# A hybrid of state-space, attention and delta-rule layers: the gated linear units of both state-space layers as seven half-size products, and three smaller changes

## The chip, the core and the metric

The kernel runs on one core of one Trainium2 chip. The metric is the device time of one execution in microseconds (us); lower is better. The kernel before takes 4232.0 us, the median of three runs (4231.37 to 4232.86). All numbers are 32-bit floats. TensorE (PE) multiplies, VectorE (DVE), ScalarE (ACT) and GpSimd (POOL) do the rest, SyncE (SP) starts most weight loads.

## The reference

512 tokens of width 2048 pass through two layers of a first block and one layer of a second block.

```python
for l in range(2):                                  # the first block
    mod = silu(c) @ w_ada[l] + b_ada[l]             # shift, scale, gate: 6144 columns
    h = rms_norm(x, norm_g[l]) * (1 + scale) + shift
    u, z_s, q, k, v, z_a = split(h @ w_in[l])       # each 1024 wide
    y = gelu(state_space(u))                        # 512 x 1024
    ab = y @ w_glu[l] + b_glu[l]                    # 1024 x 2048: the gated linear unit
    y_s = ab[:, :1024] * sigmoid(ab[:, 1024:]) * silu(z_s)
    y_a = diff_attention(rope(q), rope(k), v) * silu(z_a)
    x = x + gate * (concat(y_s, y_a) @ w_out[l])
...
# the second block: one layer, its own modulation
q_a, k_a, v_a, z_a, b_a, a_a, q_b, k_b, v_b, z_b, gl_a, gl_b = split(h @ w_in_2)
beta = sigmoid(b_a)                                 # 8 heads: 8 columns
g = -exp(a_log) * softplus(a_a + dt_bias)           # 8 columns
...                                                 # gated delta rule, in chunks
bias = rel_bias[t5_bucket(dist)]                    # 16 heads, a band of 128 distances
logits = where(valid, q_b @ k_b.T * scale + bias, -inf)   # sliding window
```

## The kernel before

The program is planned first: generators append steps to one list, and every engine then walks this list and issues its own part of each step in the list's order. So the order is written out by hand, through generators that are interleaved at fixed rates, and each engine's queue is in order: an instruction that waits holds up all that stand behind it on its engine.

Activations lie transposed in two regions (features on partitions, 512 tokens along). A weight block of 1 MB goes into one of four slots (`wring`). A matrix product is a job for 256 output columns. `dense` (L539) computes it as two tiles of 128 columns by 512 tokens, each a chain of matmuls over the 128-row pieces of the inner dimension. `fast` (L491) computes the same job from seven products of half size (128 columns by 256 tokens over half of the inner dimension) instead of eight; PE takes them in the order 1, 2, 4, 6, 5, 7, 3 (`seventh`, L1478). DVE makes for it four sums of weight halves (`w_sum`, L1957), which product 7, products 5 and 6, and product 3 need, per operand once the sums of its quarters (`quarter_sums`, L2006), and puts the products together (`fold`, L1980) in six operations; product 7 also waits for the first fold. ACT copies one product out between (`set_by`). In the kernel before, `fast` is used for the output projection of layer 1 and for most of the second block; the gated linear unit uses `dense`.

A 32-bit matmul is two instructions in the profile, so that 256 instructions of 128x512 are the 128 matmuls of one layer's unit.

The unit (`glu`, L1003) has eight jobs per layer, in pairs: one for 256 gate columns (ACT takes the Sigmoid of each tile, DVE multiplies with z) and one for the matching output columns (DVE multiplies them by the gate). They stand at the end of `beside_attention` (L931), the filler that is interleaved with `attention` (L949) at 1.6 filler steps per attention step for the first 32 steps and then 45/37. A filler step is what a job issues between two `yield`s: for `dense` four matmuls of 128x512, for `fast` one half-size product. The attention handles 8 heads with four query blocks each ("units"); one unit has two steps: PE makes the scores (`k,q`), DVE masks and takes the maximum (`soften`), ACT the exponential, DVE weighs the two maps (`weigh`), PE transposes the weights (`const,tring`).

At each filler step `carry` (L464) also moves the modulation of later layers (`modulation`, L600) on by 1.7 of its steps: POOL fetches a piece of `w_ada` into `side`, DVE adds it times c into a sum (`ada_sum`, a SCALAR_TENSOR_TENSOR `tring<-side,cact,tring`), and when a sum over 16 pieces is complete PE adds it over the partitions: four matmuls with a single column of ones (`ada_turn`, L1532) into a bank that the modulation holds until its end.

The second block begins with two groups of conv products. Then come 16 columns for b_a and a_a as a job of their own (`ba`): ACT copies the result, PE turns it, ACT takes the Sigmoid, DVE computes the decay (`gates`, L2451). After it come the window's values (`vb`, 64 matmuls of 128x256 with the tokens on the output's partitions), and then products for the delta rule, with one step of `make_band` (L1102) per product: for each of 16 heads PE spreads a column of `rel_bias` over 128 partitions and 384 distances, DVE adds the mask and POOL stores it.

## Time and profile before

| | |
|---|---|
| median of three runs | 4232.0 us |
| the profiled execution | 4236.4 us |
| its span | 4234.6 us |
| PE busy | 4106.9 us, 97% of the span |
| DVE busy | 2264.3 us, 53% |
| ACT, POOL busy | 811.7 us, 498.3 us |

The profile is of one execution. Busy time is the time in which an engine executes; PE's matmuls are pipelined, so the mean duration of one is longer than the distance between two. The chain that ended last is 87% PE and 8% DVE.

### The profile page before, as it was taken

The numbers are of one execution on the slowest core, as the hardware profiler recorded it, in microseconds if no ns is written. First come the engines' busy times: TensorE is split into PE (matmuls) and PEld (weight loads), VectorE is DVE, ScalarE is ACT, GpSimd is POOL, SyncE is SP. The second block draws the span as 40 slices with busy tenths as digits, with TensorE's granted clock in tenths as the row PEclk, the third lists the DMA queues.
The fourth block names the chain that finished last, engine by engine and source line by source line (L and its number), as shares of the span: only waits on it lengthen the run. The fifth ranks groups of instructions, "written<-read, shape, count | busy, mean of one in ns | idle before, by whom it ended". The sixth has DMA issues, their size and how long they took to land.

```text
span 4234.6 us, 41304 instructions
## 1 busy us (share of the span) xinstructions
PE 4106.9 (97%) x16042; PEld 2753.4 (65%) x16042; DVE 2264.3 (53%) x4157; ACT 811.7 (19%) x1481; POOL 498.3 (12%) x816
## 2 busy tenths in 40 slices
PE   6999999999999999999999999999999999999999
PEld 3665544444446555444458757888888888888888
DVE  5666536664523664355656535555555347665643
ACT  2222201132011222011221222222221123320000
POOL 0243111111111332111111000000000011100000
PEclk8999999999999999999999999999999999999999
DMA  9533332434552333324345232121212243424423
GB/s 327 197 120 105 109 127 94 130 110 152 149 168 86 114 105 112 127 92 129 109 144 167 92 123 82 60 75 60 75 60 75 75 131 125 140 87 150 133 95 105
DMA packets 370193, 499.29 MB, mean 118 GB/s; under 512 B 44380, under 2 KB 279119, under 8 KB 369487
## 3 DMA queue, kind: packets, MB, share of 16 engines
q1 hardware_dynamic: 289984, 340.16, 24.8%
q0 software_dynamic: 38608, 125.86, 9.4%
q10 hardware_dynamic: 41406, 30.63, 2.3%
q8 instruction: 127, 2.08, 0.2%
q14 instruction: 68, 0.55, 0.0%
HBM read 462.51 MB, written 34.08 MB: 117 GB/s over the span
## 4 chain that ended last, share of the span: by engine, by line
PE 87%; DVE 8%; ACT 2%; DMA 2%; issue 1%; ACTq 0%; POOL 0%; DVEq 0%; SPq 0%; POOLq 0%
PE bank L108 84%; PE bank L111 2%; DVE tring L123 2%; DVE tring L129 2%; ACT tring L116 1%; DMA side<-in_w_ada 1%; DVE wring L123 1%; DVE bank L123 0%; DVE dring L123 0%; DVE tring L126 0%; ACT L116 0%; DVE dring L126 0%; DVE s_delta L123 0%; DMA yaT<-in_w_ada 0%; ACT L120 0%
## 5 line engine op out<-in xcount | busy, mean ns | idle before, releaser
L108 PE MATMUL bank<-region_b,wring 128*128 128x256 f32 (+2 forms) x4448 | 1322.6, 451 | 5.0 <-ACT region_b L116 3.9
L108 PEld LDWEIGHTS bank<-region_b,wring 128*128 128x128 f32 (+1 forms) x4448 | 829.5, 190 | 409.4 <-issue 330.1
L108 PE MATMUL bank<-region_a,wring 128*128 128x256 f32 (+1 forms) x3232 | 1070.9, 484 | 1.6 <-DVE wring L123 1.6
L108 PEld LDWEIGHTS bank<-region_a,wring 128*128 128x128 f32 x3232 | 604.7, 191 | 384.3 <-issue 338.7
L153 POOL DMA_DIRECT2D side<-in_w_ada x384 | 209.0, 545 | 1306.1 <-DVE tring L129 937.0
L129 DVE SCALAR_TENSOR_TENSOR tring<-side,cact,tring 128x512 f32<-128x512 f32 x360 | 302.9, 841 | 78.2 <-DMA side<-in_w_ada 41.3
L123 DVE TENSOR_TENSOR tring<-bank,tring 128x256 f32<-128x256 f32 (+1 forms) x229 | 101.0, 441 | 317.9 <-PE bank L108 314.8
L108 PE MATMUL bank<-wring,region_b 128*128 128x512 f32 (+1 forms) x640 | 263.5, 568 | 7.2 <-ACT region_b L116 7.2
L123 DVE TENSOR_TENSOR wring<-wring 128x1024 f32<-128x1024 f32 (+1 forms) x213 | 234.8, 1102 | 19.8 <-PE bank L108 10.9
L108 PE MATMUL bank<-wring,region_a 128*128 128x512 f32 x512 | 227.9, 603 | 4.4 <-ACT region_a L116 4.4
L116 ACT ACTIVATE tring<-bank 128x512 f32<-128x512 f32 (+1 forms) x166 | 81.3, 492 | 777.9 <-PE bank L108 470.3
L108 PEld LDWEIGHTS bank<-wring,region_b 128*128 128x128 f32 x640 | 150.3, 238 | 113.8 <-issue 84.8
L123 DVE TENSOR_TENSOR tring<-bank,side 32x512 f32<-32x512 f32 (+1 forms) x160 | 110.1, 688 | 175.2 <-PE bank L108 171.2
L116 ACT ACT_TABLE_LOAD x111 | 142.4, 1283 | 308.4 <-DVE sring L126 252.4
L108 PEld LDWEIGHTS bank<-wring,region_a 128*128 128x128 f32 x512 | 126.6, 250 | 97.5 <-issue 67.9
L108 PE MATMUL bank<-yaT,wring 128*128 128x512 f32 (+1 forms) x512 | 170.6, 486 | 0.0
L123 DVE TENSOR_TENSOR bank<-bank,tring 128x256 f32<-128x256 f32 (+1 forms) x213 | 110.2, 517 | 84.2 <-PE bank L108 81.7
L123 DVE TENSOR_TENSOR tring<-tring 128x512 f32<-128x512 f32 (+2 forms) x142 | 98.7, 695 | 88.8 <-ACT tring L116 83.2
L116 ACT ACTIVATE tring<-bank,sring 128x128 f32<-128x128 f32 (+3 forms) x128 | 67.3, 526 | 410.9 <-DVE sring L126 410.8
L108 PEld LDWEIGHTS bank<-yaT,wring 128*128 128x128 f32 x512 | 97.1, 190 | 66.9 <-issue 60.3
L116 ACT ACTIVATE tring<-tring 128x512 f32<-128x512 f32 x145 | 88.0, 626 | 254.7 <-DVE tring L126 189.6
L111 PEld LDWEIGHTS bank<-const,tring 128*128 128x128 f32 (+1 forms) x474 | 55.8, 142 | 77.0 <-issue 45.5
(285 smaller groups left out, 4312.0 us busy)
## 6 DMA issues: line engine op xcount, KB each, us to landing
wring<-in_w_in SPq DMA_DIRECT2D x180, 1024.0 KB, 5.3
side<-in_w_ada POOLq DMA_DIRECT2D x384, 256.0 KB, 3.2
wring<-in_w_out SPq DMA_DIRECT2D x48, 1024.0 KB, 8.5
yaT<-in_w_ada SPq DMA_DIRECT2D x16, 1024.0 KB, 9.3
wring<-in_w_glu SPq DMA_DIRECT2D x16, 1024.0 KB, 8.1
tring<-x_saved SPq DMA_DIRECT2D x48, 256.0 KB, 2.9
gring<-in_w_ada POOLq DMA_DIRECT2D x43, 256.0 KB, 3.0
SS<-in_w_ada SPq DMA_DIRECT2D x8, 1024.0 KB, 9.5
```

The lines of the kernel that those rows point to most:

```text
L108: return self.e.matmul(*a, **k) if self.e else self
L111: return self.e.transpose(*a) if self.e else self
L116: return self.e.activation(o, x, f, **k) if self.e else self
L123: return self.e.tensor_tensor(*a) if self.e else self
L129: return self.e.scalar_tensor_tensor(out=o, in0=a, scalar=s, in1=b, op0=op0, op1=op1) if self.e else self
L153: return self.e.dma_start(dst, src, allow_slow_non_contiguous=True) if self.e else self
```

## The change

1. The gated linear units of both layers use `fast`. The operand's quarters are summed into the region of h, which is free once the layer's last projection is done (`lambda: [full(last, 1)]`). The rates of `interleave` and `carry` are as before, while a job now has seven filler steps where it had four.
2. `ada_turn` transposes the sum (four transposes) into a bank of its own, and DVE adds along the free axis (`ada_total`).
3. The 16 columns for b_a and a_a are fetched beside the 256 of the values, whose matmuls become 272 wide; `gates` moves behind them.
4. The band of all 16 heads is made by a single matmul (a partition for each of 16 heads, eight times over), one addition and eight stores.

```diff
-        return 4 if self.n > 256 else 8
+        return 4 if self.width > 256 else 8
+
+    @property
+    def width(self):
+        return self.n + (self.more[1] if self.more else 0)
...
             def turn(n0):
+                aux.take("ada_turn", m, n0)
                 do("ada_turn", m, n0)
                 temps.give("acc", m, n0)
+
+            def total(n0):
+                do("ada_total", m, n0)
+                aux.give("ada_turn", m, n0)
...
         def glu(l):
             wg = d["w_glu"][l]
 
+            last = len(jobs) - 1
+            parts = Split(f"glu{l}", HT, lambda r, k, n: xTs[l][:, HT + HT // 2 * r + k:HT + HT // 2 * r + k + n, :], lambda k: [ssm_d.of("yT", l, k)],
+                          [pairs_of(hTs[l][:, 2 * i:2 * i + 2, :]) for i in range(4)], lambda: [full(last, 1)], {})
+            quarter(parts, 0, 4)
+            do("quarter_rest", parts, 0, 4)
+
             def y_dense(n0, use):
-                return Dense(wg, HT, n0, 256, False, lambda k: xTs[l][:, HT + k, :], lambda k: [ssm_d.of("yT", l, k)], use, (l, n0 % HALF // P))
+                return Dense(wg, HT, n0, 256, False, None, parts.ready, use, (l, n0 % HALF // P), parts, lay[l]["s3_glu"])
...
-                yield from dense(y_dense(HALF + n0, "glu_gate"))
-                yield from dense(y_dense(n0, "glu_out"))
+                yield from fast(y_dense(HALF + n0, "glu_gate"))
+                yield from fast(y_dense(n0, "glu_out"))
...
-        run_all(dense(layer_dense(2, w_two, OFF["ba"], "keep_ba", n=2 * GH)))
...
-        do("gates")
...
+        vb_job = layer_dense(2, w_two, OFF["vb"], "keep_v2", tokens="blocks")
+        vb_job.more = (OFF["ba"], 2 * GH)
+        run_all(dense(vb_job))
+        do("gates")
...
-        interleave(gdn_products(0, 2), make_band(), 1)
+        aux.take("band")
+        temps.take("band")
+        do("band")
+        aux.give("band")
+        temps.give("band")
+        run_all(gdn_products(0, 2))
...
             def ada_turn(m, n0):
...
-                    i = pe.matmul(bank[:, c:c + 1], acc[:, j * P:(j + 1) * P], ones[:, 0:1], start=True, stop=True)
+                    i = pe.transpose(bank[:, j * P:(j + 1) * P], acc[:, j * P:(j + 1) * P], ident)
...
+            def band_():
+                place = temps.at("band")
+                room(aux.clear("band"))
+                pe.wait_ge(*att_d.of("rel_bias"))
+                pe.matmul(aux.at("band")[:, 0:SW_W], place[0:32, SW_W:SW_W + P], K("hot")[0:32, :], start=True, stop=True).then_inc(
+                    *scored.up("band"))
...
+            def ada_total(m, n0):
+                bank, l, c = aux.at("ada_turn", m, n0), mods[m][0], n0 // P
+                dve.wait_ge(*ada_turned.of(m, n0))
+                dve.reduce_sum(mod[:, l, c:c + 4], bank[:, :].rearrange("p (j k) -> p j k", j=4), AX).then_inc(*ada_ready.up("total", m, n0))
...
             def gates_():
+                dve.wait_ge(*taken_a.of("beta", TT - 1))
...
             def keep_v2(jid, j, l):
                 dve.wait_ge(*full(jid, j))
...
+                dve.tensor_tensor(gates[:, 7, j, :], bank[:, 256 + GH:256 + 2 * GH], hp[:, 1, :], AD).then_inc(*taken_d.up("decay_in", j))
+                dve.tensor_copy(temps.at("vb", j)[:, 0:256], bank[:, 0:256]).then_inc(*taken_d.up("vb", j))
...
+            def keep_v2(jid, j, l):
+                room(passed("h2"))
+                act.wait_ge(*taken_d.of("vb", j))
+                act.activation(gates[:, 1, j, :], banks.at(jid, j)[:, 256:256 + GH], ACT.Sigmoid).then_inc(*taken_a.up("beta", j))
...
+                for r in range(8):
+                    pool.dma_start(band_dram[:, 16 * r:16 * r + 16, :], temps.at("band")[16 * r:16 * r + 16, 0:SW_W].unsqueeze(1).broadcast_to(
+                        [16, 16, SW_W])).then_inc(*band_out.landing())
```

How the change moves instructions is seen in the order in which they stand on an engine. A row is the operation, output<-inputs, the shape and how many of the same follow each other; here a matmul counts once.

PE at the start of layer 0's gated linear unit, before (`region_a` holds its operand, `const,tring` are the transposes of attention weights, `k,q` its scores):

```order
L108 MATMUL bank<-region_a,wring 128x512 x4
L111 MATMUL bank<-const,tring 128x128 x2
L108 MATMUL bank<-region_a,wring 128x512 x8
L108 MATMUL bank<-k,q 128x512 x2
L108 MATMUL bank<-region_a,wring 128x512 x4
L111 MATMUL bank<-const,tring 128x128 x3
```

The same place after (`region_b` holds the sums of quarters, `s_glu` the weights of product 7):

```order
L108 MATMUL bank<-region_a,wring 128x256 x4
L111 MATMUL bank<-const,tring 128x128 x2
L108 MATMUL bank<-region_a,wring 128x256 x4
L108 MATMUL bank<-region_b,wring 128x256 x4
L108 MATMUL bank<-k,q 128x512 x2
L108 MATMUL bank<-region_b,wring 128x256 x4
L111 MATMUL bank<-const,tring 128x128 x3
```

Between two attention instructions about as many filler steps stand as before, each with half the columns.

DVE at that place before, from the end of the last finished head (`yaT`) to the next unit's mask (`const_one`):

```order
L129 SCALAR_TENSOR_TENSOR yaT<-tring,vec,yaT 128x512
L129 SCALAR_TENSOR_TENSOR tring<-side,cact,tring 128x512
L123 TENSOR_TENSOR tring<-tring 128x512
L129 SCALAR_TENSOR_TENSOR tring<-side,cact,tring 128x512 x2
L138 RECIPROCAL sring<-sring 128x1 x2
L126 TENSOR_SCALAR tring<-tring,sring,small 128x384
L129 SCALAR_TENSOR_TENSOR tring<-tring,sring 128x384
L123 TENSOR_TENSOR bank<-bank,const_one 128x128
```

And after:

```order
L129 SCALAR_TENSOR_TENSOR yaT<-tring,vec,yaT 128x512
L123 TENSOR_TENSOR region_b<-region_a 128x1024
L123 TENSOR_TENSOR region_b<-region_a,region_b 128x1024 x2
L123 TENSOR_TENSOR region_b<-region_a 128x1024
L123 TENSOR_TENSOR s_glu<-wring 128x512
L123 TENSOR_TENSOR wring<-wring 128x4x128
L129 SCALAR_TENSOR_TENSOR tring<-side,cact,tring 128x512
L123 TENSOR_TENSOR wring<-wring 128x4x128
L129 SCALAR_TENSOR_TENSOR tring<-side,cact,tring 128x512
L123 TENSOR_TENSOR wring<-wring 128x4x128
L129 SCALAR_TENSOR_TENSOR tring<-side,cact,tring 128x512
L138 RECIPROCAL sring<-sring 128x1 x2
```

Four sums of quarters and four sums of weights stand between the head's end and the weighing of the next unit (RECIPROCAL and what follows it).

PE between the conv products and the first delta-rule products of the second block, before (`tring,ones` are sums of squares for a norm):

```order
L108 MATMUL bank<-tring,ones 128x512
L108 MATMUL bank<-region_b,wring 16x512 x4
L111 MATMUL bank<-const,tring 128x16 x4
L108 MATMUL bank<-wring,region_b 128x256 x64
L108 MATMUL bank<-region_b,wring 128x256 x8
L108 MATMUL bank<-const_two,relb 128x384
L108 MATMUL bank<-region_b,wring 128x256 x8
L108 MATMUL bank<-const_two,relb 128x384
```

After:

```order
L108 MATMUL bank<-tring,ones 128x512
L108 MATMUL bank<-wring,region_b 128x272 x4
L108 MATMUL bank<-tring,ones 128x512
L108 MATMUL bank<-wring,region_b 128x272 x52
L108 MATMUL bank<-const_two,tring 128x384
L108 MATMUL bank<-region_b,wring 128x256 x16
L108 MATMUL bank<-region_a,wring 128x256 x16
```

The job of 16 columns and 15 of 16 band matmuls are gone; the one that is left stands ahead of the products, behind the gates.

## Rows read from the trace of the kernel before

**Rows 1.** The page's busy times: busy us, share of the span, instructions.

```profile
PE 4106.9 (97%) x16042; PEld 2753.4 (65%) x16042; DVE 2264.3 (53%) x4157; ACT 811.7 (19%) x1481; POOL 498.3 (12%) x816
```

**Rows 2.** Stretches: from:to length, busy us (instructions) of each engine, PE clock, DMA.

```profile
895.80:1038.20 142.40, 140.00 (x385) 63.26 (x384) 75.70 (x165) 46.79 (x83) 17.39 (x31) 1.00 0.46 148
2066.20:2204.90 138.70, 136.65 (x385) 63.33 (x384) 75.95 (x165) 47.23 (x83) 16.82 (x30) 1.00 0.48 152
905.35:1002.00 96.65, 96.51 (x270) 42.93 (x269) 55.34 (x132) 39.47 (x71) 10.74 (x20) 1.00 0.44 144
```

**Rows 3.** PE's timeline, layer 0's unit: start, us, operation, instructions [idle before].

```profile
901.78 0.41 PE L111 MATMUL bank<-const,tring 128*128 128x128 f32 x2 [2.27 <-DVE tring L129]
1006.41 0.60 PE L111 MATMUL bank<-const,tring 128*128 128x128 f32 x4
...
1016.73 17.33 PE L108 MATMUL bank<-region_a,wring 128*128 128x512 f32 x40
1033.90 0.95 PE L108 MATMUL bank<-ones,tring 128*128 128x1 f32 x8
```

**Rows 4.** PE's timeline in the last projection, which is made of half-size products.

```profile
4099.15 10.52 PE L108 MATMUL bank<-mixed,wring 128*128 128x256 f32 x48
4109.51 3.62 PE L108 MATMUL bank<-mixedT,wring 128*128 128x256 f32 x16
```

**Rows 5.** Groups of DVE instructions by form, 3500 to 4000 us: busy, mean ns, idle before.

```profile
L123 DVE TENSOR_TENSOR tring<-bank,tring 128x256 f32<-128x256 f32 x73 | 30.9, 423 | 65.0 <-PE bank L108 64.2
L123 DVE TENSOR_TENSOR wring<-wring 128x512 f32<-128x512 f32 x42 | 29.1, 692 | 3.4
L123 DVE TENSOR_TENSOR bank<-bank,tring 128x256 f32<-128x256 f32 x49 | 20.8, 425 | 21.4 <-PE bank L108 21.4
L123 DVE TENSOR_TENSOR bank<-bank,tring 128x512 f32<-128x512 f32 x24 | 16.8, 699 | 0.8
L123 DVE TENSOR_TENSOR region_b<-region_a,region_b 128x1024 f32<-128x1024 f32 x2 | 2.5, 1226 | 0.1
```

**Rows 6.** DVE's timeline in both units.

```profile
905.42 0.75 DVE L129 SCALAR_TENSOR_TENSOR tring<-side,cact,tring 128x512 f32<-128x512 f32 x1
...
911.88 0.69 DVE L144 TENSOR_REDUCE sring<-bank 128x1 f32<-128x512 f32 x1
...
999.74 0.75 DVE L129 SCALAR_TENSOR_TENSOR region_a<-bank,vec,tring 128x512 f32<-128x512 f32 x1 [2.45 <-PE bank L108]
...
1001.25 0.75 DVE L129 SCALAR_TENSOR_TENSOR tring<-tring,sring 128x512 f32<-128x512 f32 x1
...
2073.96 0.75 DVE L129 SCALAR_TENSOR_TENSOR yaT<-tring,vec,yaT 128x512 f32<-128x512 f32 x1
```

**Rows 7.** ACT's timeline in layer 0's unit.

```profile
904.73 1.28 ACT L116 ACT_TABLE_LOAD   x1
906.03 0.69 ACT L116 ACTIVATE tring<-bank,vec 128x512 f32<-128x512 f32 x1
```

**Rows 8.** PE's timeline at the head of the second block.

```profile
2469.99 1.02 PE L108 MATMUL bank<-tring,ones 128*128 128x512 f32 x2
...
2485.55 1.10 PE L108 MATMUL bank<-tring,ones 128*128 128x512 f32 x2 [0.49 <-ACT tring L116]
...
2491.28 27.89 PE L108 MATMUL bank<-wring,region_b 128*128 128x256 f32 x128
2519.01 3.62 PE L108 MATMUL bank<-region_b,wring 128*128 128x256 f32 x16
...
2583.02 1.06 PE L108 MATMUL bank<-gates,const_two 128*128 128x8 f32 x8
```

**Rows 9.** DVE's timeline at the gates and behind them.

```profile
2492.42 0.19 DVE L123 TENSOR_TENSOR gates<-bank,headp 128x32 f32<-128x32 f32 x1 [3.66 <-ACT gates L116]
...
2498.80 0.19 DVE L129 SCALAR_TENSOR_TENSOR gates<-gates,headp 128x32 f32<-128x32 f32 x1
...
2519.67 2.36 DVE L123 TENSOR_TENSOR region_b<-region_b 128x1024 f32<-128x1024 f32 x2
```

More of the change, by code:

```diff
@@ L626, in modulation @@
                         turn(n0 - 512)
+                    if k == 8 and n0 > blocks[0]:
+                        total(n0 - 512)
             for _ in range(10):
@@ L1100, in build @@
         w_two = d["w_in_2"][0]
-        def make_band():
-            for h in range(16):
-                aux.take("band", h)
-                temps.take("band", h)
-                do("band", h)
-                aux.give("band", h)
-                temps.give("band", h)
-                yield
         def conv_job(h0, which):
@@ L1465, in mm @@
                     if job.tokens:
-                        i = pe.matmul(bank[:, 0:job.n], job.rhs(k, j), blk[:, k - k0, 0:job.n], start=k == 0, stop=k == job.kt - 1)
+                        i = pe.matmul(bank[:, 0:job.width], job.rhs(k, j), blk[:, k - k0, 0:job.width], start=k == 0, stop=k == job.kt - 1)
                     else:
@@ L1706, in values @@
                 t.then_inc(*valued.up(l, h))
-            def band_(h):
-                room(aux.clear("band", h))
-                pe.wait_ge(*two_in.all())
-                pe.wait_ge(*const_two_in.all())
-                pe.matmul(aux.at("band", h)[:, 0:SW_W], relb[0:32, h:h + 1].broadcast_to([32, P]), K("hot")[0:32, :], start=True,
-                          stop=True).then_inc(*scored.up("band", h))
-            def ba_turn():
-                bank, ba = aux.at("ba_turn"), temps.at("ba")
-                room(aux.clear("ba_turn"))
-                pe.wait_ge(*taken_a.of("ba_tile"))
-                for j in range(TT):
-                    i = pe.transpose(bank[:, 2 * GH * j:2 * GH * (j + 1)], ba[0:2 * GH, J[j]], ident[0:2 * GH, 0:2 * GH])
-                i.then_inc(*turned.up("ba"))
-                temps.leave(("ba",), pe.mine())
+            def band_():
[4 more added lines that the diff above has]
+                    *scored.up("band"))
             def gate_sums():
@@ L3058, in two_constants @@
                 act.dma_start(const_two[:, :], d["const"][:, split:]).then_inc(*const_two_in.landing())
-            def keep_ba(jid, j, l):
-                room(passed("h2"))
-                room(temps.clear("ba"))
-                act.wait_ge(*full(jid, j))
-                act.activation(temps.at("ba")[0:2 * GH, :], banks.at(jid, j)[0:2 * GH, :], ACT.Copy).then_inc(*taken_a.up("ba_tile"))
-                banks.leave((jid, j), act.mine())
-            def ba_turn():
-                bank = aux.at("ba_turn")[:, 0:2 * GH * TT].rearrange("p (j h) -> p j h", j=TT)
-                act.wait_ge(*turned.of("ba"))
-                act.activation(gates[:, 1, :, :], bank[:, :, 0:GH], ACT.Sigmoid).then_inc(*taken_a.up("ba"))
-                aux.leave(("ba_turn",), act.mine())
             def gates_():
@@ L3378, in load @@
                     *w_in[wslots.where[jid, k0]].landing(jid, k0))
+                if job.more:
+                    n0, n = job.more
+                    sp.dma_start(job_slot(jid, k0)[:, 0:job.kb, job.n:job.width],
+                                 job.w[k0 * P:(k0 + job.kb) * P, n0:n0 + n].rearrange("(k p) n -> p k n", p=P)).then_inc(
+                        *w_in[wslots.where[jid, k0]].landing(jid, k0))
                 if job.use == "glu_gate":
```

72 lines of the change are left out of this document (30 added, 42 removed).

## Prediction

> **What bounds the kernel now.** I read the page's busy times first. PE is busy for 4106.9 of 4234.6 us and DVE for 2264.3 [rows 1]: PE sets the time, so an instruction less on PE is worth its length unless something else is late there. Then the busy times by stretch. In the two stretches of the gated linear units PE is busy for 140.0 of 142.4 us and 136.65 of 138.7 us, and DVE for 75.7 and 75.95, just over half [rows 2]. The share of DVE is uneven: up to the weighing of the last unit of 512 it works 55.34 of 96.65 us. PE's timeline shows how close the two are: it already waits 2.27 us for a weighing before two transposes [rows 3], since DVE, ACT and PE take turns in every attention unit. A change that halves what PE has to do between two turns and gives DVE more of them must be summed on both engines.
>
> **The unit on PE alone.** Forty instructions of 128x512 take from 1016.73 to 1033.90 us, 0.429 us each [rows 3]; 48 of 128x256 take from 4099.15 to 4109.51, 0.2158 each [rows 4]. A layer now has 256 of the first, 109.9 us; then 8 jobs x 7 products x 8 instructions = 448 of the second, 96.7 us. PE alone would give 13.2 us per layer, 26.5 in all.
>
> **The unit on DVE.** The rates of interleaving stay, and a filler step shrinks from eight instructions of 0.429 us to eight of 0.2158. So the attention that stands beside the unit now meets about half of the PE work that covered DVE. In the order I count, for layer 0, from the end of the last finished head (DVE at 905.4 us [rows 6]) to the third weighing of 512 (it ends at 1002.0): 27 products less one on PE, and on DVE the attention's work and 20 modulation sums, as many as before. New there are 4 sums of quarters of 1.226 (4.9 us), 16 sums of weights of 0.692 (11.1), and of the folds 9 of 0.423, 6 of 0.425 and 3 of 0.699 (8.5) [rows 5], and one sum after a turn, which I price like the 0.69 of a reduction over 512 [rows 6]. Two multiplications by z and four gated outputs leave the stretch, since fewer jobs end in it: 2 x 0.69 (an addition of 512 [rows 5]) and 4 x 0.75 [rows 6] = 4.4. So DVE has 55.3 + 4.9 + 11.1 + 8.5 + 0.7 - 4.4 = 76.1 us of work. PE has in the same stretch its 26 products, 44.9 us, and about 20 us of attention: 65. DVE is the bound there, by 11 us before any wait.
>
> To that come DVE's own waits. The two gate jobs that end in the stretch let DVE wait for a Sigmoid: 1.28 for the table, which the attention's exponentials push out, and 0.69 [rows 7], then 0.8 for the second tile, 2.8 each, 5.6 us. Following both orders by hand I find 1.9 us more where a fold or a mask waits for a product or a score, and the distances between some 150 short instructions add about 5.3 over busy time. Together 88.9 us: the third weighing ends at 994.3.
>
> On PE then stand the transposes (0.4), 30 products (51.8), a head's values (2.2), a norm's sum (1.0) and two turns (0.9): 56.3 us; DVE has some 50 us there, nearly as much, and each gate job's Sigmoid delays the next sum of weights a little: 1.5 us. Layer 0's unit ends at 1052.1 us where it ended at 1038.2: 13.9 us later. Layer 1: DVE starts at 2074.7 (2073.96 + 0.75 [rows 6]), has 0.8 us more of work, and a rest with fewer modulation sums (waits of 1.0): 2074.7 + 89.7 + 56.3 + 1.0 = 2221.7 against 2204.9 [rows 2], 16.8 later; I take off 1 because no modulation sums are left ahead of the output projection's weight sums. **The units cost 29.7 us.** From below: without any wait and gap, 905.4 + 76.1 + 56.3 = 1037.8 and 2074.7 + 76.9 + 56.3 = 2207.9: 2.6 us in all. From above: every wait twice as long as I found (7.5 + 1.5 and 7.5 + 1.0 more), some 47.
>
> What this does to the queues: the sums of quarters stand ahead of four sums of weights and the weighing of 384 on DVE, and PE's product 4 and the transposes behind it wait for them; the first PE wait should be 5 us (product 4 is due at 903.8, the third sum ends at 909.1). POOL and the fetches of `w_ada` follow DVE and are not late by my walk.
>
> One rule would make it dearer. ACT's row has the table load at 904.73 and the Sigmoid at 906.03, 1.30 us later [rows 7]: nothing stands between them. The Trainium skill ("ScalarE: Activation LUTs", section "What ACT_TABLE_LOAD costs") adds a drain of about 1380 ns to each change of set. By that rule the four gate jobs in the two DVE-bound stretches would cost 5.5 us more, by the row nothing, and I go by the row.
>
> **The modulation turns.** The order has 28 turns in either kernel; 24 stood outside the units, 22 do now. A turn by ones takes 0.95 us, one by four transposes of 128x128 takes 0.60 [rows 3]: 24 x 0.95 - 22 x 0.60 = 9.6 us saved. The others are in the sums above. DVE's 28 additions of 0.69 lie beside PE's projections, where DVE has slack; if that cover were gone they would cost up to 15 us, and the stretch shares say it is not. Bound: 8 to 11 us saved.
>
> **Head of the second block.** Three things on PE, all from [rows 8].
> - Out: from the first sum of squares (2469.99) to the values job (2491.28) are 21.3 us, of which the four sums of squares stay. In their place: the sums keep the pace that ACT sets (2469.99, then up to 2485.55), and four matmuls of the values fit in each gap; after the last one at 2486.5 stand 104 instructions. An instruction of 272 columns should take 0.2158 x 272/256 = 0.229: the values end at 2510.4 instead of 2519.0.
> - In: the gates now follow the values on DVE, and PE's one band matmul waits behind them. An addition and a copy (0.7), the Sigmoid and the table for the exponential (about 2), the chain from 2492.42 to 2498.80 less its first wait (5.3), the two last sums of quarters (2.36) [rows 9], a copy of the bias (0.3) and the matmul itself (0.9): PE starts the next product at about 2521.8, 2.8 us later than now. Queued behind the band on DVE are the sums of weights; they are due 10 us later, after three raw products.
> - Out: the 16 band matmuls. From 2519.01 to 2583.02 are 64.0 us for 14 products of 16 instructions (48.4): 15.6 us.
> Together 12.8 us saved. If the gates took only as long as PE's wait for weights, 15; if ACT and DVE took turns more slowly, 8.
>
> **The sum.** 29.7 - 9.6 - 12.8 = +7.3 us. The profiled execution took 4236.4 us, 4.4 above the median (its span 4234.6 lies 1.8 inside it), so it would take 4243.7; on the median it is **4239.3 us**.
>
> **Rivals.** Less than 0.2% (8.5 us) can hardly be told from no change by a measurement of this kernel.
> - DVE's waits are covered: the gaps and Sigmoids fall where DVE was ahead anyway, and the units cost their lower bound. 2.6 - 22.4 = -19.8: 4212. For: DVE was idle for 41 of 96.65 us. Against: that was PE's covering work, of which half is gone, and the sum of instructions alone leaves nothing to gain.
> - The half-size products pay in full, because attention doesn't follow DVE's order as tightly as I think: -26.5 - 22.4: 4183. For: PE is busy 97%. Against: the wait of 2.27 us with DVE at 58%.
> - Slower, by the tail of the units: there PE has 51.8 us of products and DVE about 50 us with 24 modulation sums in layer 0, each of which needs its fetch of 256 KB. If the fetches come late the sums of weights behind them do too, and every product 6 waits. It decides once a job's DVE work passes 12.1 us, which is a single wait of half a microsecond; 2 us a job on 7 jobs adds 14: 4253.
> - Slower, at the head of the second block: the band matmul waits for a fence or a store ahead of it, and the three parts give 5 instead of 12.8: 4247.
>
> **How the numbers follow.** My forecast 0.48 (own range 4229 to 4248), waits covered 0.16, full payment 0.04, late tail 0.22, slow gates 0.10. Faster by over 0.2% (below 4223.5) are the second and third case: 0.20. Within 0.2% (to 4240.5) lies a little over half of the forecast and some of the gates' case and of the waits': 0.37. Slower: 0.43. The range reaches down to the middle of the covered case and up past the late tail: 4217 to 4256.
>
> **What the profile after would show.** Unit: a stretch from the first 128x256 product to the output projection of about 156 us in layer 0, DVE near 90% busy up to the last weighing, PE waiting some 25 us for DVE's `tring`, `wring` and `region_b`; if PE is at 98% there and the stretch is 129 us, the full payment was right. Turns: 0.60 or less each. Head of the second block: a PE wait of about 11 us ahead of the one band matmul, released by DVE. I am wrong in the main point if PE's idle time in the two units stays below 15 us.

## Result: slower, 4262.5 us where 4239.3 were forecast

The changed kernel takes 4262.5 us (median of 4 runs, 4260.0 to 4263.8) against 4232.4 of the kernel before on the same chip: ratio 1.0068, 95% interval 1.0055 to 1.0081, some 30 us slower. The direction was forecast, the size not: the time lies outside the range. The profiled execution took 4261.5 us (span 4259.7), 25.1 more than the one of before.

The page's busy times after, to hold against [rows 1]:

```profile
PE 4068.4 (96%) x16248; PEld 2818.7 (66%) x16248; DVE 2366.6 (56%) x4342; ACT 797.8 (19%) x1484; POOL 496.0 (12%) x808
```

PE has 38.5 us less to do and the kernel takes 25 us longer, so PE stands still for 64 us more. Where, the stretches tell; each unit is parted at the last four transposes of attention weights, behind which DVE has no more weighing. The columns are those of [rows 2]:

```profile
890.07:986.82 96.75, 76.76 (x296) 54.41 (x295) 83.86 (x186) 30.34 (x69) 13.00 (x23) 0.84 0.37 112
986.82:1059.76 72.94, 65.92 (x279) 52.42 (x278) 53.28 (x88) 9.18 (x14) 15.70 (x30) 0.98 0.66 209
2077.87:2176.79 98.92, 75.49 (x295) 53.30 (x294) 84.47 (x187) 30.24 (x69) 13.10 (x23) 0.86 0.41 127
2176.79:2243.51 66.72, 62.77 (x279) 52.34 (x278) 48.81 (x80) 9.06 (x14) 9.13 (x17) 0.97 0.49 152
```

Layer 0's unit takes 169.7 us where it took 142.4, layer 1's 165.6 where it took 138.7: +27.3 and +26.9. In the first part of each DVE is busy for 84 of 97 to 99 us, PE for 76 only; and the granted clock, 1.00 everywhere in [rows 2], is 0.84 and 0.86. PE's timeline of layer 0's unit shows both:

```profile
896.04 0.66 PE L111 MATMUL bank<-const,tring 128*128 128x128 f32 x2 [3.97 <-DVE tring L129]
...
903.38 3.75 PE L108 MATMUL bank<-region_b,wring 128*128 128x256 f32 x8 [3.26 <-DVE region_b L123]
...
950.56 1.09 PE L111 MATMUL bank<-const,tring 128*128 128x128 f32 x4 [3.25 <-DVE tring L129]
951.44 3.62 PE L108 MATMUL bank<-region_b,wring 128*128 128x256 f32 x8
...
1003.85 0.60 PE L111 MATMUL bank<-const,tring 128*128 128x128 f32 x4
...
1015.80 3.72 PE L108 MATMUL bank<-region_b,wring 128*128 128x256 f32 x16 [2.71 <-DVE wring L123]
...
1034.24 3.25 PE L108 MATMUL bank<-region_b,s_glu 128*128 128x256 f32 x8 [2.47 <-DVE bank L123]
```

Eight instructions of a product take 1.89 us at full clock; at 903.38 and 951.44, behind waits, they take 3.75 and 3.62, which is the lower of the clock's two levels. The row at 1003.85 is a modulation turn: 0.60 where it was 0.95.

The head of the second block, PE, against [rows 8]:

```profile
2504.04 1.02 PE L108 MATMUL bank<-tring,ones 128*128 128x512 f32 x2
...
2509.36 2.03 PE L108 MATMUL bank<-tring,ones 128*128 128x512 f32 x2 [2.47 <-ACT tring L116]
...
2519.91 2.04 PE L108 MATMUL bank<-tring,ones 128*128 128x512 f32 x2 [5.92 <-ACT tring L116]
...
2526.22 24.00 PE L108 MATMUL bank<-wring,region_b 128*128 128x272 f32 x104
2560.31 1.61 PE L108 MATMUL bank<-const_two,tring 32*128 32x384 f32 x2 [10.09 <-DVE tring L132]
2561.85 9.90 PE L108 MATMUL bank<-region_b,wring 128*128 128x256 f32 x32
...
2620.18 5.13 PE L108 MATMUL bank<-region_b,wring 128*128 128x256 f32 x23
```

From the first sum of squares to the product behind the gates' sums it takes 116.1 us where it took 122.7 (2469.99 to 2592.72 in the trace before): 6.6 saved, 12.8 forecast. The forecast's own stretch ends earlier, at the gates' sums (2583.02 before, 2613.03 after): 109.0 us where it was 113.0, so 4.0 of the 12.8 came. The other 2.6 us lie in the gates' sums, where three rows of eight took 1.87, 2.05 and 1.82 us before and take 1.06, 1.13 and 1.06 now. The band's wait is there as forecast. Ahead of it ACT does not keep its pace: PE waits 5.92 us for a square that ACT could not make, because DVE stood at the sums of quarters, which the order puts ahead of the last conv units:

```profile
2508.84 1.22 DVE L123 TENSOR_TENSOR region_a<-region_b 128x1024 f32<-128x1024 f32 x1
...
2518.42 0.68 DVE L129 SCALAR_TENSOR_TENSOR qkv<-tring 128x512 f32<-128x512 f32 x1
```

All else of the profile (start, modulation turns, the rest) is 22.5 us shorter, where 9.6 were forecast: 54.2 - 6.6 - 22.5 = +25.1.

### The profile page after: what moved, and what is told of

Its sections match the earlier page's. It is cut to its first block, busy times and chain, and to the rows that moved or that the text cites. A ratio compares the mean times of both kernels' runs of the same rounds, so it can differ in the third digit from the quotient of the medians.

```text
span 4259.7 us, 41958 instructions
## 1 busy us (share of the span) xinstructions
PE 4068.4 (96%) x16248; PEld 2818.7 (66%) x16248; DVE 2366.6 (56%) x4342; ACT 797.8 (19%) x1484; POOL 496.0 (12%) x808
## 4 chain that ended last, share of the span: by engine, by line
PE 82%; DVE 12%; ACT 2%; DMA 2%; issue 1%; ACTq 0%; DVEq 0%; POOL 0%; SPq 0%
PE bank L108 80%; DVE tring L129 2%; PE bank L111 2%; DVE tring L123 2%; DMA side<-in_w_ada 1%; ACT tring L116 1%; DVE wring L123 1%; DVE bank L123 1%; DVE tring L126 1%; DVE region_b L123 0%; DVE dring L123 0%; DVE sring L144 0%; DVE region_a L123 0%; DVE dring L126 0%; ACT L116 0%
## 5 line engine op out<-in xcount | busy, mean ns | idle before, releaser
L108 PE MATMUL bank<-region_b,wring 128*128 128x256 f32 (+1 forms) x4544 | 1293.8, 439 | 14.3 <-ACT region_b L116 5.2
L108 PEld LDWEIGHTS bank<-region_b,wring 128*128 128x128 f32 x4544 | 860.0, 193 | 369.8 <-issue 270.3
L108 PE MATMUL bank<-region_a,wring 128*128 128x256 f32 (+1 forms) x3360 | 1050.0, 466 | 11.3 <-DVE wring L123 5.5
L108 PEld LDWEIGHTS bank<-region_a,wring 128*128 128x128 f32 x3360 | 635.1, 193 | 355.5 <-issue 289.3
L123 DVE TENSOR_TENSOR tring<-bank,tring 128x256 f32<-128x256 f32 (+1 forms) x277 | 121.3, 438 | 376.1 <-PE bank L108 372.6
L123 DVE TENSOR_TENSOR wring<-wring 128x1024 f32<-128x1024 f32 (+1 forms) x261 | 267.9, 1027 | 28.2 <-PE bank L108 16.5
L123 DVE TENSOR_TENSOR bank<-bank,tring 128x256 f32<-128x256 f32 (+1 forms) x261 | 134.9, 517 | 83.6 <-PE bank L108 80.6
L111 PE MATMUL bank<-const,tring 128*128 128x128 f32 x582 | 95.1, 281 | 41.4 <-DVE tring L129 22.6
L111 PEld LDWEIGHTS bank<-const,tring 128*128 128x128 f32 x582 | 69.5, 142 | 93.5 <-issue 70.8
```

Source lines behind the costliest of these rows:

```text
L108: return self.e.matmul(*a, **k) if self.e else self
L111: return self.e.transpose(*a) if self.e else self
L123: return self.e.tensor_tensor(*a) if self.e else self
```

## Experiments

Ratios are to the kernel before on the same chip, with their 95% intervals. Differences from another changed kernel are those of the medians, which come from several chips; the kernel before took 4232.4 to 4234.4 us on them. The letters of the theories run through all expectations.

### What each part is worth

**units_only**, the kernel before and:

```diff
-                yield from dense(y_dense(HALF + n0, "glu_gate"))
-                yield from dense(y_dense(n0, "glu_out"))
+                yield from fast(y_dense(HALF + n0, "glu_gate"))
+                yield from fast(y_dense(n0, "glu_out"))
```

with the sums of quarters and the tile that this needs.

> The kernel before with the gated linear units of both layers as half-size products and nothing else. In the trace after, the two units take 169.7 and 165.6 us where they took 142.4 and 138.7: PE waits 25 us more in each, its instructions there take 15 us longer at a granted clock of 0.90, and 13 us of products are gone. Theory A (the units alone lose the time, and the clock falls because PE waits there): +54 us, 4286 us, granted clock of both units about 0.90. Theory B (the low clock comes from elsewhere in the changed kernel, or the three smaller changes lose the time; the units cost what the forecast said): +30 us, 4262 us, with a clock near 1.0 in the units.

Measured: 4272.5 us, 1.0089 (1.0074 to 1.0104), +39. The profiled execution took 4279.1 and shows both units much as the changed kernel does: 165.3 and 164.7 us. The clock is 0.94 there, between A's 0.90 and B's 1.0, and 0.89 and 0.90 in the first parts. So the low clock comes with the units (A), and they alone lose the time. A's 54 were too many for the median: +39, or 43 by the profiled one.

**three_only**, the changed kernel with the diff above turned round.

> The changed kernel with the gated linear units by dense products as before: only the modulation turns, the gates' inputs beside the values and the band in one matmul. From the trace after: a turn takes 0.43 us of PE's time where it took 0.81, 28 turns save 10.6; the head of the second block up to the gates' sums is 6.6 us shorter. Theory A: the units alone lose, so 4232.4 - 10.6 - 6.6 - 2 = 4213 us. Theory B (the loss sits in these three): above 4232 us.

Measured: 4211.7 us, 0.9949 (0.9937 to 0.9962), -21.9. A holds to 1.3 us. The forecast's sum for these three, -22.4, holds too, but by luck: the turns alone give 15.2 where it had 9.6 (next run), and the head gives less than its 12.8. The units then add 51 to it in the changed kernel but 39 to the kernel before. In the trace of units_only the two units are 48.9 us longer than before and all the rest is 6.2 us shorter, though nothing else was changed; no run here settles why.

**turns_only**, the kernel before with `ada_turn` by transposes and `ada_total`.

> The kernel before with the modulation turns by four transposes and a sum on DVE, and nothing else. In the traces a turn holds PE for 0.43 us where it held it for 0.81, and there are 28. Theory A (the turns save what they take): -10.6 us. Theory E (the three smaller changes without the units gave -21.8, of which the head of the second block shows -6.6 and the turns explain 10.6; the rest is a bank that the modulation no longer holds for its whole length, and would show here too): -15 us.

Measured: 4218.5 us, 0.9965 (0.9953 to 0.9978), -15.2. E's number, but not its reason as far as the traces go: 28 x 0.38 = 10.6 is the turns' own. The rest is seen at two places in layer 1's state space. Before, PE waits 2.46 us for ACT at 1419.56, and the next eight instructions of 128x512 take 5.30 us instead of 3.60; in this trace neither is there. And behind a wait of 2.06 us, which both traces have, eight instructions take 3.72 us where they took 5.41. In the changed kernel the first wait is back (2.90), with no slow row behind it. So a part of the gain hangs on how two engines happen to meet.

### How many sums DVE has to make in the units

**pace_mod**, the changed kernel and:

```diff
+            carried[0] = 1.7 * 4 / 7
             quarter(parts, 0, 4)
```

> The changed kernel, with the modulation moved on by 0.97 of its steps per filler step in the units instead of 1.7, so that it makes as many sums beside a job as before the change (a job has seven filler steps where it had four). This takes some 40 sums of 0.75 us, 30 us of DVE's work, out of layer 0's unit, which has 137 us of it in 170. Theory A (DVE is the bound of the units; PE's waits and the clock follow from it): 7 us less in the attention's stretch and 8 to 10 in the tail, in each layer: about 4232 us. Theory C (PE waits for the turn that attention's own chain DVE, ACT, DVE takes, and the sums only fill DVE's idle time): 4258 us or more.

Measured: 4243.5 us, 1.0024 (1.0015 to 1.0033): 19 less than the changed kernel, short of A's 30, far from C. Its stretches, parted like those above:

```profile
891.80:982.23 90.43, 73.19 (x295) 52.21 (x294) 77.15 (x176) 30.31 (x69) 8.26 (x14) 0.87 0.33 104
982.23:1047.30 65.07, 63.51 (x276) 50.83 (x275) 45.28 (x76) 9.06 (x14) 9.67 (x18) 1.00 0.56 179
2065.67:2158.72 93.05, 74.09 (x295) 53.20 (x294) 77.77 (x176) 30.42 (x69) 8.75 (x15) 0.89 0.35 111
2158.72:2219.75 61.03, 59.85 (x276) 50.91 (x274) 44.58 (x74) 9.06 (x14) 8.07 (x15) 1.00 0.49 155
```

Ten instructions fewer on DVE, 6.7 us of its time, and layer 0's first part is 6.3 us shorter; in layer 1 6.7 and 5.9. PE had 20 and 23 us of idle time there before and has 17 and 19 still. That is what a bound looks like: the stretch follows DVE's work nearly one for one. The two units are 25.7 us shorter together and the profiled execution 19.0: some 7 us come back elsewhere, and the traces don't say where.

**tail_pace**: the same line, but ahead of the fifth job (`if n0 == 512`).

> The changed kernel with the modulation's pace of 0.97 instead of 1.7 steps per product only from each unit's fifth job on, which is past the attention's last weighing. With the slow pace in the whole unit (pace_mod) layer 0's stretch up to the last transposes of weights was 6.3 us shorter with 6.7 us less DVE work in it, the tail behind it 7.8 us shorter; in layer 1 5.9 and 5.7; 7 of these 26 us were given back later. Theory L (each part of the unit answers to its own sums: in the stretch DVE is the bound one for one, in the tail PE waits for sums of weights and folds that stand behind modulation sums): the stretches stay at 96.8 and 98.9 us, the tails fall from 72.9 and 66.7 to about 65 and 61, and the kernel takes about 4252 us. Theory M (the tail's waits come from a backlog that DVE carries over from the stretch): the tails keep their waits of 7.0 and 3.8 us, 4260 us.

Measured: 4243.5 us, 1.0026 (1.0016 to 1.0035), 19 less than the changed kernel, more than L's 10:

```profile
889.47:985.02 95.55, 73.07 (x296) 51.74 (x295) 83.29 (x185) 30.35 (x69) 12.64 (x23) 0.91 0.37 113
985.02:1049.59 64.57, 63.52 (x276) 50.84 (x275) 46.28 (x78) 9.07 (x14) 10.73 (x20) 1.00 0.62 196
2064.28:2158.39 94.11, 74.02 (x295) 52.30 (x294) 82.64 (x183) 30.35 (x69) 13.09 (x23) 0.89 0.37 116
2158.39:2220.88 62.49, 60.35 (x275) 50.84 (x274) 46.96 (x79) 9.07 (x14) 9.16 (x17) 1.00 0.58 189
```

Layer 0 does as L says: first part nearly as before, tail 64.6 instead of 72.9, its waits 1.0 us instead of 7.0. M falls: nothing is carried over. In layer 1 the tail is 4.2 us shorter; its first part is 4.8 shorter with 1.8 less DVE work, which L did not foresee, and of which 3 us have no cause shown (that the modulation stands at another point by then is a guess). Nothing was given back. So the tail's waits were made by modulation sums ahead of sums of weights and folds, and going by the median their removal is worth as much as that of all the sums. A part of it was their fetches: in the changed kernel DVE waits 5.5 and 5.6 us in the tails for pieces of `w_ada`, in tail_pace never. The longest such wait stands right ahead of the fold that PE waits for at 1034.24:

```profile
1032.77 0.75 DVE L129 SCALAR_TENSOR_TENSOR tring<-side,cact,tring 128x512 f32<-128x512 f32 x1 [3.58 <-DMA side<-in_w_ada]
...
1033.77 0.42 DVE L123 TENSOR_TENSOR bank<-bank,tring 128x256 f32<-128x256 f32 x1
```

How much of the tail the sums cost by their own length and how much by their fetches, no run separates.

**pace_both**, as pace_mod, and the attention moved on by four of a job's seven products:

```diff
+        def four_of_seven(g):
+            for n, _ in enumerate(g):
+                if n % 7 in (1, 3, 5, 6):
+                    yield
...
-                yield from fast(y_dense(HALF + n0, "glu_gate"))
+                yield from four_of_seven(fast(y_dense(HALF + n0, "glu_gate")))
```

and so for the output jobs.

> The changed kernel with both paces as before the change: 0.97 modulation steps per product, and the attention moved on by four of a job's seven products, so that as much PE work stands between two steps of the attention as before. Theory A (half the cover was the cause): PE's waits in the units fall from 27 us to 10 or less in each, the granted clock there rises above 0.95, and the kernel takes about 4215 us; with no waits at all 4190. Theory D (the folds and sums of weights bind DVE in any order, since 98 us of DVE's work then stand beside 102 of PE's): about 4235 us, as with the modulation's pace alone.

Measured: 4246.0 us, 1.0029 (1.0018 to 1.0041). D rather than A, though D's 4235 is 11 too low: the clock is up to 0.95 and 0.97, as A says, but with the old cover PE still waits 24.9 us in layer 0's unit and 24.7 in layer 1's. Of these 6.93 and 6.83 are for the sums of quarters alone. In layer 0 these are ready 13.3 us after the unit's start, as in the changed kernel, where PE's wait for them was 3.26 because 3.97 had been spent before the transposes.

**tail_two**, half-size products for the last two jobs of each unit only:

```diff
+                if n0 < 768:
+                    yield from dense(y_plain(HALF + n0, "glu_gate"))
+                    yield from dense(y_plain(n0, "glu_out"))
+                else:
+                    if n0 == 768:
+                        carried[0] = 1.7 * 4 / 7
+                        quarter(parts, 0, 4)
+                        do("quarter_rest", parts, 0, 4)
```

> The changed kernel with the first six jobs of each unit dense and only the last two as half-size products, when the attention is over or nearly; the modulation's pace is 0.97 steps per product there. Theory A (half-size products pay 1.65 us a job wherever DVE has slack and nothing of the attention stands between): 4 jobs x 1.65 = 6.6 us less than the three smaller changes alone (4211.7), so about 4205 us. Theory G (the sums of quarters and the sums of weights make PE wait at any place in the unit): 4212 us or more.

Measured: 4221.6 us, 0.9972 (0.9959 to 0.9984), 10 more than three_only. G: the sums cost more than four jobs save, even where the attention is over.

```profile
999.93 3.02 PE L108 MATMUL bank<-region_b,wring 128*128 128x256 f32 x8 [2.20 <-DVE region_b L123]
1002.74 3.00 PE L108 MATMUL bank<-wT,v 128*128 128x512 f32 x8
...
1020.62 5.41 PE L108 MATMUL bank<-region_b,wring 128*128 128x256 f32 x16 [1.89 <-DVE wring L123]
```

These are layer 0's: two waits, and behind each rows at the lower clock (3.02 for 1.89, 3.00 for 2.32, 5.41 for 3.62): 4.1 us and 3.6, against 3.3 saved. In layer 1 the same two waits are longer, 5.5 us in sum, and the rows behind them have full speed:

```profile
2169.23 1.96 PE L108 MATMUL bank<-region_a,wring 128*128 128x256 f32 x8 [2.62 <-DVE region_a L123]
...
2189.55 3.72 PE L108 MATMUL bank<-region_a,wring 128*128 128x256 f32 x16 [2.89 <-DVE wring L123]
```

### What the clock costs

**stalls**, the kernel before with three waits in layer 0's output projection:

```diff
+        STALLS = {256: 1, 768: 4, 1280: 10}
...
+            def stall(n0, jid):            # PE
+                pe.wait_ge(*att_d.of("stall", n0))
...
+                dve.wait_ge(*full(jid, 1))            # DVE
+                dve.memset(place[:, :], 0.0).then_inc(*d_step.up())
+                for n in range(STALLS[n0]):
+                    own()
+                    dve.tensor_tensor(place, place, place, AD)
```

> The kernel before, with three waits put into layer 0's output projection, where PE otherwise has none: behind its second, fourth and sixth job PE waits until DVE has seen the job's end, done its own step, cleared a tile and added it to itself 1, 4 and 10 times (0.69 us each). The waits should be about 2.2, 4.3 and 8.5 us, 15 in sum. Theory A (PE's clock is granted lower right behind a wait of over 2 us): in the next 10 us behind each a row of matmuls at nearly twice its length and a granted clock of 0.7 to 0.9, 2 to 4 us each: 4233.6 + 15 + 9 = about 4257 us. Theory H (the low clock of the units has to do with what runs there, half-size products and a busy DVE): instructions of 0.429 us right behind each wait, 4249 us.

Measured: 4262.7 us, 1.0068 (1.0054 to 1.0081), +29.

```profile
1091.06 8.83 PE L108 MATMUL bank<-region_a,wring 128*128 128x512 f32 x16 [4.48 <-DVE tring L123]
...
1163.28 8.82 PE L108 MATMUL bank<-region_a,wring 128*128 128x512 f32 x16 [6.94 <-DVE tring L123]
...
1231.23 8.98 PE L108 MATMUL bank<-region_a,wring 128*128 128x512 f32 x16 [10.17 <-DVE tring L123]
```

The same sixteen instructions take 7.03 us elsewhere. So the three waits (21.6 us, longer than I meant) cost 1.8, 1.8 and 1.95 us on top, and a wait of 10 us hardly more than one of 4. My expectation had overlooked that the output projection already has a wait, 3.72 us at 1104.80 in the trace before; the sixteen instructions behind it take 8.73 us in both kernels. H falls: no half-size products run here, and DVE is busy for only 6.7 of the 30 us behind the three waits. The Trainium skill ("TensorE: Matmul & The Clock Gate", section "What's actually happening") has the throttled state as the default, which activity releases; the rows agree.

**warm**, the changed kernel with unread matmuls ahead of eleven of the units' waits:

```diff
+        FILL = {("w_turn", 0, 5, 1): 5, ("w_turn", 1, 5, 1): 5, ("p4", 0): 4, ("p4", 1): 4, ("root", 0, 5): 3, ("root", 1, 5): 3,
+                ("w_turn", 0, 6, 3): 4, ("w_turn", 1, 6, 3): 6, ("scores", 0, 7, 3): 4, ("scores", 1, 7, 3): 6, ("w_turn", 0, 7, 2): 2}
...
+                for _ in range(FILL[place]):
+                    i = pe.matmul(aux.at("fill", *place)[:, :], ident, xTs[l][:, HT, :], start=True, stop=True)
```

> The changed kernel with matmuls of 128x512 that nobody reads, into a free bank, ahead of eleven places in the two units where PE waits 2.3 to 4.6 us: 22 of them in layer 0 and 24 in layer 1, 0.43 us each, so many per place that a wait of 1.1 to 2.2 us is left. What PE waits for is unchanged (DVE and ACT). Theory A (the lower clock behind a wait comes from PE standing still): the 20 us of extra work lie inside the waits and cost nothing, the clock stays up, and the 1.8 us that each such wait costs on top (the waits in the output projection showed 1.75 to 1.9) come back at eleven places: 4262.5 - 20 = about 4243 us. Theory I (the clock falls in the units whatever PE does in its waits, or what a wait for DVE costs is not the clock): 4262 us, or up to 4282 if the extra work adds to the path.

Measured: 4265.8 us, 1.0074 (1.0060 to 1.0088): not faster than the changed kernel's 1.0068. The first parts of the two units:

```profile
890.97:989.12 98.15, 85.46 (x339) 56.01 (x338) 84.06 (x186) 30.31 (x69) 13.18 (x24) 0.98 0.38 115
2078.92:2178.07 99.15, 87.56 (x343) 56.95 (x342) 84.17 (x187) 30.20 (x69) 13.10 (x23) 0.97 0.39 122
```

The filling did what A says of the clock: it is 0.98 and 0.97 where it was 0.84 and 0.86, and PE's rows have their full speed (951.86 1.89 us for eight, 3.62 before). It gave next to nothing back: the parts are 98.2 and 99.2 us long, 96.8 and 98.9 before, with DVE busy for the same 84 us.

The two lengths alone would not prove it, for the filling was heavier than planned. An unread matmul is two instructions of 0.429 us, which I had counted as one; and the ones ahead of the last unit's scores could only start when the wait that they were to fill was over:

```profile
973.68 5.40 PE L108 MATMUL bank<-region_a,const 128*128 128x512 f32 x8 [4.13 <-DVE bank L123]
979.01 1.13 PE L108 MATMUL bank<-k,q 64*128 64x512 f32 x4
```

They put 5.3 us (layer 1: 7.3) ahead of the scores. But up to them the comparison is clean, and after them it is DVE's walk that tells. PE reaches this place 82.7 and 82.7 us after the units' start, where it was 82.5 and 84.7, at a clock of 1.00 and 0.98 instead of 0.86 and 0.87. DVE then waits 0.69 and 2.80 us for the late scores, and still ends the third weighing after 95.1 and 97.3 us, where it was 95.2 and 97.0. Without these two waits it would have ended 0.8 and 2.6 us earlier than in the changed kernel; that is my estimate of what the clock is worth in the first parts. Where DVE is the bound, a faster PE waits longer. PE's busy time there, without the filling's 18.9 and 20.6 us, is 66.6 and 67.0 us where it was 76.8 and 75.5. My theory that the clock had added 31 us to the units is wrong in nearly all of these 19 us of it.

### The head of the second block

**head_order**, three_only and:

```diff
+        for n, _ in enumerate(dense(vb_job)):
+            if n == 6:
+                for k in range(0, HT, 4):
+                    quarter(h_parts, k, 4)
+                    do("quarter_rest", h_parts, k, 4)
+            if n == 12:
...
+                do("band")
...
+        for n, _ in enumerate(gdn_products(0, 2)):
+            if n == 3:
+                do("gates")
```

> The three smaller changes with dense units, and at the head of the second block another order on DVE: the sums of quarters behind the last conv unit (inside the values job), the band ahead of the last tile of values, the gates behind the first product's three halves. In the changed kernel PE waits there 2.47 + 5.92 + 0.90 us for ACT's squares, which wait for DVE, and 10.09 us for the band, and its granted clock is 0.84 over 58 us. Theory A (both waits come from the order on DVE, and the clock falls because of them): waits of 2.5 and 0 to 1 us in their place and some 5 us from the clock, 18 to 22 us less than the three smaller changes alone (4211.7): about 4192 us. Theory F (the ACT engine's table loads set the pace of the squares whatever stands on DVE): only the band's wait goes, 4200 us or more.

Measured: 4219.5 us, 0.9963 (0.9951 to 0.9976), 8 more than three_only. A was right on both waits (2.46, 0.50 and 2.19 us for ACT, none for the band), and a third one came out from under them:

```profile
2499.31 3.62 PE L108 MATMUL bank<-region_b,wring 128*128 128x256 f32 x16
2524.31 5.11 PE L108 MATMUL bank<-region_b,wring 128*128 128x256 f32 x16 [21.39 <-DMA wring<-in_w_in]
```

The job of 272 columns takes four slots of four pieces each where 256 columns took two, so that the next weights can only be fetched when it ends. In three_only 15 us at 315 GB/s were hidden by the wait for the band; here the band's stores ran beside the fetches.

**head_late**: the band moved behind the first job (`if n == 7` in the last loop).

> The three smaller changes with dense units and the head of the second block in a third order: the sums of quarters inside the values job as in head_order, the gates behind the third product of the first job, the band and its eight stores (3.1 MB) behind that job. In head_order PE waited 21.4 us for the second weight block of the first product: the values' 272 columns hold all four weight slots to their end, and the band's stores, which start at the same time as the next fetches, share the DMA engines with them. Theory J (the stores are what delays the fetch): the wait is 3 us or less, and with ACT's squares 6 us earlier and no wait for the band the kernel takes about 4199 us. Theory K (the four slots alone delay the fetch, stores or not): a wait of 8 us or more, about 4207 us.

Measured: 4201.4 us, 0.9922 (0.9910 to 0.9935), 10 less than three_only: J. There is no wait for weights left, and one of 4.77 us ahead of the band:

```profile
2506.30 7.07 PE L108 MATMUL bank<-region_a,wring 128*128 128x256 f32 x32
...
2531.95 1.61 PE L108 MATMUL bank<-const_two,tring 32*128 32x384 f32 x2 [4.77 <-DVE tring L132]
```

This is the fastest version of the study, 33 us under the kernel before: the three smaller changes, dense units and this order.

## Why the prediction was wrong, step by step

**PE alone, and DVE as the bound of the first part: right.** DVE's walk to the third weighing of 512 was to take 98.5 us from the unit's start in layer 0 (994.3 less 895.8) and 98.2 in layer 1. The weighings end at 985.25 and 2174.92, 95.2 and 97.0 us after the start: 4.5 us less in both together.

```profile
984.50 0.75 DVE L129 SCALAR_TENSOR_TENSOR tring<-tring,sring 128x512 f32<-128x512 f32 x1
...
1053.88 0.75 DVE L129 SCALAR_TENSOR_TENSOR region_a<-bank,vec,tring 128x512 f32<-128x512 f32 x1
```

PE's idle time in the two units is 54 us where my test was 15, and the waits forecast at the start (5 us before product 4) are 3.97 and 3.26.

**The step that failed: from the third weighing to the unit's end, and what that end was compared with.** Two faults, 10.3 and 17.6 us.

First, the 29.7 us itself: "layer 0's unit ends at 1052.1 us where it ended at 1038.2" compares two different points. My 1052.1 is the end of the unit's last product. 1038.2 is the start of the instructions on `yaT`, and ahead of them stand the projection's first sixteen on `region_a` and a modulation turn. DVE's last output of the unit in the trace of before shows that PE was done with it by then:

```profile
1030.67 0.75 DVE L129 SCALAR_TENSOR_TENSOR region_a<-bank,vec,tring 128x512 f32<-128x512 f32 x1 [5.26 <-PE bank L108]
```

To the same point my walk would have had to go on by sixteen of 0.429, 6.9 us. In layer 1 it is sixteen half-size ones, 3.4. Like against like, the forecast for the units was 40.0, not 29.7, and the time 4249.6.

Second, the tail. I gave PE 56.3 us of work and 1.5 (layer 1: 1.0) of waits. Measured to the last product's end (1059.76 - 6.87 and 2243.51 - 3.45) it took 67.6 and 65.1, so 9.8 and 7.8 more. In layer 0 5.5 of this are waits (7.0, for sums of weights and a fold), 1.6 the product that PE was in when the weighing ended, 1.8 rows at the lower clock (the one at 1034.24 and the next); 0.9 is left over. In layer 1 waits are 2.8 of it, the product that PE was in 1.9, a row at the lower clock 1.7 (5.41 us at 2218.61, where 3.72 is the full speed); 1.4 is left over. "POOL and the fetches of `w_ada` follow DVE and are not late by my walk" failed here too: DVE waits 5.5 and 5.6 us for them in the tails. The rival with the late tail had this mechanism, the late fetches included, at 14 us and a chance of 0.22; on like points its sum would have been 4263. I had counted DVE's 50 us for the tail nearly right (53.3 and 48.8) and then drawn the wrong conclusion from 50 beside 56: so close together, the order inside a job decides. tail_pace shows it: with fewer modulation sums the tail's waits are gone.

**The clock.** I never priced it, and after the result took it for the cause. The stalls show its price where PE is the bound, 1.8 us a wait; warm shows that in the parts where DVE is the bound it is next to nothing, by estimate 0.8 us in layer 0 and 2.6 in layer 1. It counts for a few us in the tails, and at the head of the second block, where 32 instructions of this size take 7.07 us at full speed and the 32 behind the band now take 9.90.

**Turns: mechanism right, size low.** By durations in a row I took 0.95 and 0.60, by distances between starts it is 0.81 and 0.43; outside the units 24 x 0.81 - 22 x 0.43 = 10.0 where I had 9.6. All 28 give 10.6; measured alone, 15.2.

**Head of the second block: 4.0 in the forecast's own stretch, instead of 12.8.** "The sums keep the pace that ACT sets" failed: their four took 21.3 us (2504.04 to 2525.29) where they took 15.6, since I had not walked DVE's order there, in which 9.6 us of quarter sums stand ahead of what ACT waits for. That is 5.8 of the 8.8 us missing, up to the end of the values (46.2 us where I had 40.4); 2.8 are the row of 9.90. The gates' term held: 10.09 us of wait for 11 forecast. What the wait hides, the fetch of the next job's weights, I had not seen.

**The table load.** Loads with an instruction right behind, 1.29 us later each (2506.06 and 2507.35, 2509.24 and 2510.53 in ACT's timeline after), show no drain. Going by the row was right.

```profile
2506.06 1.28 ACT L120 ACT_TABLE_LOAD   x1
2507.35 0.69 ACT L116 ACTIVATE tring<-bank,const 128x512 f32<-128x512 f32 x1
2508.07 1.15 ACT L116 ACTIVATE tring<-tring 128x512 f32<-128x512 f32 x2
2509.24 1.28 ACT L116 ACT_TABLE_LOAD   x1
2510.53 0.63 ACT L116 ACTIVATE tring<-tring 128x512 f32<-128x512 f32 x1
```

**What is open.** The profile's remaining 22.5 us (9.6 forecast): some 10 are turns outside the units, 3.0 lie ahead of 150 us, where PE waits for the first weights, and two rows at the lower clock, of 1.7 us each, fell away at waits that are there in both traces (the eight instructions at 1341.18 took 5.41 us before). I can't place the other 6. All of this but the turns, and the 2.6 us at the gates' sums, is 15 us shorter without a term in the forecast. It made the miss smaller, by luck: the terms that it did have were 33 us too low together (24.5 for the units, 8.8 for the head, and 0.4 the other way for the turns).

## What to carry to other kernels

Products of half size save PE an eighth and ask DVE for sums in exchange; beside work that already passes from engine to engine, sum both engines for each part of the stretch, and where they come as close as here (50 us beside 56), walk the order instead. Compare ends only at the same instruction: a time read out of a timeline tells where a row starts, not what stands ahead of it. And before taking a wait away, find out what else landed while it lasted.

## What the runs showed of the hardware

- Behind each of the three waits of 4.5 to 10.2 us in the output projection PE ran at the lower clock for a while, at 1.8 to 1.95 us of loss, whatever the wait's length. Waits of 2 to 3 us were followed by such rows in some places and executions and not in others (2.06 us at 1340.26 of before: eight instructions in 5.41 us; the same wait at 1335.26 in turns_only: 3.72; in tail_two 1.89 us with and 2.89 us without).
- Matmuls that nobody reads, in place of standing still, kept the granted clock of a stretch at 0.98 instead of 0.84 (layer 1: 0.97 instead of 0.86), and the stretch was no shorter.
- Weight fetches beside eight stores of 384 KB moved 250 GB/s together, with the DMA engines 95% busy (head_order, 2495 to 2525); without the stores it was 315 at 96% (three_only, 2495 to 2510).
- Loads of ACT's tables took 1.28 us, and the next instruction started 1.29 us after the load did.
